# A gated DeltaNet and Mamba-2 decoder step on one core: GpSimd's order of halves and masks in the GDN loop is changed

## What is computed

```python
a_mat = einsum("bnhid,bnhjd->bnhij", k * beta, k) * decay * strict
t_mat = triangular_solve(eye + a_mat, eye, lower=True, unit_diagonal=True)   # the inverse
u = t_mat @ (v * beta);  w = t_mat @ (k * beta * exp(g))
...
v_new = u_c - w_c @ S
o = qd_c @ S + qk_c @ v_new
S = S * exp(gl_c) + kd_c.T @ v_new
```

## Time and profile before

| | us |
|---|---|
| median of 3 runs | 2419.1 (2417.37 to 2422.41) |
| profiled execution, its own time | 2417.6 |
| its span in the trace | 2415.8 |
| PE busy | 2326.3 |
| POOL busy | 1794.2 |
| DVE busy | 1614.2 |
| ACT busy | 1276.5 |

### The profile page before, as it was taken

One profiled execution on the slowest core, in us unless ns is written; L12 is line 12 of the kernel. 1 busy time (PEld: TensorE's weight loads), 2 busy tenths in 40 slices (PEclk: granted clock), 3 DMA queues, 4 the chain that ended last, 5 costly groups with the idle time before them and its releaser, 6 DMA issues.

```text
span 2415.8 us, 59306 instructions
## 1 busy us (share of the span) xinstructions
PE 2326.3 (96%) x21792; PEld 2183.8 (90%) x21792; DVE 1614.2 (67%) x3159; ACT 1276.5 (53%) x2236; POOL 1794.2 (74%) x2284
## 2 busy tenths in 40 slices
PE   5899999999999999999999979999999999999997
PEld 5799999999999999989999978999999999899997
DVE  7667666666666676761217576998999989703375
ACT  4555555555555555543335456555555555433453
POOL 5566566565555556558889968888898889798896
PEclk9999999999999999999999989999999999999999
DMA  5444444444444444436444446766576657454443
GB/s 200 154 155 151 157 155 151 149 150 145 146 154 149 145 144 147 145 125 223 149 167 151 158 148 211 228 202 206 199 245 215 194 196 239 174 195 157 153 156 118
DMA packets 126776, 410.89 MB, mean 170 GB/s; under 512 B 21344, under 2 KB 37984, under 8 KB 122112
## 3 DMA queue, kind: packets, MB, share of 16 engines
q1 hardware_dynamic: 80784, 294.49, 35.2%
q10 hardware_dynamic: 45936, 115.64, 14.1%
HBM read 363.47 MB, written 46.61 MB: 170 GB/s over the span
## 4 chain that ended last, share of the span: by engine, by line
POOL 37%; PE 34%; issue 22%; DVE 4%; ACT 1%; POOLq 0%; DMA 0%; DVEq 0%; ACTq 0%
POOL wl L336 36%; PE psj L381 10%; PE psj L383 10%; PE psj L382 10%; POOL h L344 1%; PE psA L773 1%; PE psE L403 1%; PE psE L747 1%; PE psA L721 1%; DVE h L2012 0%; DVE arena L1535 0%; DVE xl L1819 0%; DVE xl L1460 0%; PE psB L727 0%; ACT xh L845 0%
## 5 line engine op out<-in xcount | busy, mean ns | idle before, releaser
L336 POOL TENSOR_TENSOR wl<-ring,wh 128x256 fp32r<-128x256 f32 x2232 | 1760.9, 824 | 600.4 <-ACT wh L826 599.8
L381 PE MATMUL psj<-xh,wh 128*128 128x288 f32 x4400 | 1357.9, 309 | 31.7 <-DVE xl L1460 16.5
L382 PE MATMUL psj<-xl,wh 128*128 128x288 f32 x4400 | 1305.7, 297 | 0.0
L383 PE MATMUL psj<-xh,wl 128*128 128x288 f32 x4400 | 1301.0, 296 | 0.0
L381 PEld LDWEIGHTS psj<-xh,wh 128*128 128x128 f32 x4400 | 831.3, 189 | 83.1 <-issue 43.9
L826 ACT ACTIVATE wh<-ring 128x1024 fp32r<-128x1024 f32 x558 | 586.5, 1059 | 583.8 <-PE psj L383 535.1
L382 PEld LDWEIGHTS psj<-xl,wh 128*128 128x128 f32 x4400 | 833.7, 189 | 1.9
L383 PEld LDWEIGHTS psj<-xh,wl 128*128 128x128 f32 x4400 | 834.6, 190 | 0.0
L907 ACT ACTIVATE arena<-psj 128x256 f32<-128x256 f32 x112 | 42.7, 381 | 190.7 <-PE psj L383 185.0
L1811 DVE TENSOR_TENSOR h<-h,psj 128x288 f32 x32 | 14.6, 455 | 155.7 <-PE psj L383 155.7
L1885 DVE SCALAR_TENSOR_TENSOR arena<-arena 128x256 f32<-128x256 f32 x144 | 110.7, 796 | 3.4
(11 more groups left out here) (346 smaller groups left out, 2965.4 us busy)
## 6 DMA issues: line engine op xcount, KB each, us to landing
ring<-weights_d SPq DMA_DIRECT2D x558, 512.0 KB, 3.3
h<-gstate_d ACTq DMA_DIRECT2D x16, 1024.0 KB, 6.1
gst_s_d<-h ACTq DMA_DIRECT2D x16, 1024.0 KB, 3.9
h<-sstate_d ACTq DMA_DIRECT2D x32, 512.0 KB, 5.4
sst_s_d<-h ACTq DMA_DIRECT2D x32, 512.0 KB, 5.0
arena<-g_rows_d ACTq DMA_DIRECT2D x16, 864.0 KB, 6.0
arena<-s_rows_d ACTq DMA_DIRECT2D x8, 1152.0 KB, 8.6
h_spill_d<-h ACTq DMA_DIRECT2D x2, 2304.0 KB, 7.5
```

Of the source, the lines that this page charges most:

```text
L336: ins = pool.tensor_tensor(wl[:, s, n:n + 2], ring[:, s, n:n + 2], wh[:, s, n:n + 2].bitcast(F32), ALU.subtract)
L381: pe.matmul(out, w_h, xh[:, kt, :], start=(kt == 0), stop=False)
L382: pe.matmul(out, w_h, xl[:, kt, :], start=False, stop=False)
L383: mm = pe.matmul(out, w_l, xh[:, kt, :], start=False, stop=(kt == KT - 1))
```

## The change

Two things in GpSimd's program for the GDN loop. The sample masks are written ahead of the fifth half of weights (k=4), not behind it. And ahead of the seventh half (k=6) GpSimd waits until VectorE has ended the inverse of the same iteration (`g_de` at m * 6 + 6). This wait stands in the loop over m = 0 to 14; the last iteration is written out behind the loop, without it. GpSimd computes the same things from the same data.

```diff
             pool.wait_ge(S("spill"), 16)
-            with pool.Fori(0, GH) as m:
+            def gdn_halves(m, hold):
+
                 for k in range(12):
                     hc = 2 * T_GLOOP + k
-                    lower(m * 12 + (hc + 1), hc % 4)
                     if k == 4:
                         sample_masks(m)
+                    if hold and k == 6:
+                        pool.wait_ge(S("g_de"), m * 6 + 6)
+                    lower(m * 12 + (hc + 1), hc % 4)
+
+            with pool.Fori(0, GH - 1) as m:
+                gdn_halves(m, True)
+            gdn_halves(GH - 1, False)
             at = 2 * T_GLOOP + 12 * GH
```

## The result

| | before | after |
|---|---|---|
| median, us | 2419.1 (2417.37 to 2422.41) | 2448.58 (2446.8 to 2451.8) |
| profiled execution, its own time | 2417.6 | 2451.8 |
| its span | 2415.8 | 2450.0 |
| period of the GDN loop | 62.94 | 64.23 to 64.27; five of 65.8 |
| rest of TensorE before L545 / L552, start to start | 0.22 | 1.84, 15 times |

The ratio of after to before is 1.0121, with a 95% interval of 1.011 to 1.0132: slower by 29.5 us. The lines of the kernel after are 7 higher than those of before: L545 is now L552, L1618 is L1625, L1703 is L1710, L1609 is L1616, L1533 and L1535 are L1540 and L1542, and L383 is L390.

A forecast was written before the change was run, and what follows sets the result against it. TensorE, busy for 96% of the span, was taken to bound the kernel. -4.6 + 30.2 + 4.5 = +30.1 us on the profiled 2417.6 gave 2447.7, and 2449 us as median; range 2428 to 2467.

The forecast's parts named there:

- The masks at no cost: Masks ahead of half 4: it ends some 2.1 us later, covered by 7.7 us or more before TensorE's e=16; cost nothing.
- Level 3, -4.6: With GpSimd still, TensorE's gap at inverse level 3 shrinks from 0.55 to 0.22 us in 14 iterations: -4.6 us.
- The taps, +30.2: Behind the inverse, GpSimd's twelve instructions stretch VectorE's q/k conv taps; L545 starts 2.01 us later in 15 iterations: +30.2 us.
- The pairing of the prologue: In the prologue the same ten VectorE instructions, beside unbroken GpSimd work, take 7.39 us against 2.33 alone; taken for the loop.
- Rival 3: A smaller stall behind the inverse: two copies escape GpSimd, stall 0.9 us, 2428 us, range 2418 to 2440; chance 0.17.
- The clock, +4.5: TensorE's longer rest before L545 drops its clock in one iteration of five: 3 x 1.5 = +4.5 us; bounds 0 and 23.
- What is late next, hidden: Later halves, SP's refill and taps j=2,3 (some 0.9 us late) stay hidden from TensorE; if not, up to 13 us more.
- The sum: All terms together: +30.1 us on the profiled 2417.6 gives 2447.7; the median, 1.5 above, 2449 us.
- That the clock falls in most iterations: Rival: 10 to 15 falls of TensorE's clock give +15 to +23 in place of 4.5, 2459 to 2468 us; chance 0.11.
- That the taps hide: Rival: taps end by 186.99, stretched by less than 3.05 us, L545 doesn't wait, only -4.6 stays: 2414.5 us; chance 0.08.
- Strict turns: Rival: each of the ten taps waits for a whole GpSimd instruction, 9.33 us, stall 3.95, +55, 2474 us; chance 0.02.

The follow-up runs named there:

- e4_hold_to_level4: The change, with the hold ahead of the seventh half ended earlier, by VectorE's mask of inverse level 4: 2415.75 us, ratio 0.9987 to the kernel before.
- e5_hold_to_rss: The change, with the hold ended later, by the VectorE pair that releases TensorE at e=23: 2426.88 us, ratio 1.0031 to the kernel before.
- e1_masks_only: The kernel before with the sample masks ahead of the fifth half and no hold: 2420.9 us, ratio 1.0009.
- e3_hold_eighth: The change, with the hold ahead of the eighth half (k=7) in place of the seventh: 2423.52 us, ratio 1.0022 to the kernel before.

## Why the prediction held, point by point

**The masks at no cost.** Right for the loop: 62.93 to 62.98 us a period with the masks ahead alone. Not complete: the cover that I named is that of TensorE at e=16, and I did not look at what GpSimd's pause before the fifth half was worth to VectorE in the first iteration. The masks fill this pause, and a copy that is kept waiting is then kept 2 us longer. That it is kept waiting isn't given: it happened in the profiles of the change, `e4_hold_to_level4` and `e5_hold_to_rss`, and not in those of `e1_masks_only` and `e3_hold_eighth`. How much of it is in the median stays open. All four pairs of kernels that differ in the masks' place have the one with the masks ahead at the higher median, by 1.1 to 2.4 us; against the kernel before of their own runs it is 0 to 2.2 us. The largest, of the masks alone, has an interval of 1.0 to 1.0018, and all its 11 executions are above the median of the kernel before. So a price of 1 to 2 us is likely, and the "nothing" was probably that much too low; no profile shows where it lies.

**Level 3, -4.6.** Right in place, size and count: 0.22 us in 14 iterations, 0.61 left in the last. The runs with the hold to level 4 show it as a gain by itself.

**The taps, +30.2.** The mechanism is shown, by the 12, 8 and no instructions beside the taps. The size was too large: 15 x 1.62 = 24.3. The pairing of the prologue, 7.39 us, was the nearest row there was, but in the loop the first copy escapes: it starts at 188.17, 0.03 us ahead of GpSimd, and takes 0.17 us. So 6.80 us, 0.59 less. Two links of the chain were 0.10 longer each than I had them: 194.97 to 195.10 from the taps to L1710 (I took 0.03), and 195.80 to 195.95 from there to L552 (0.05). 2.01 - 0.59 + 0.20 = 1.62. Rival 3 named this escape for both copies; it happened for one.

**The clock, +4.5.** Five falls where I chose three, each of 1.56 us where I had 1.5: 7.8 us.

**What is late next, hidden.** Right. No second stall at e=24 or e=27. The taps j=2 and 3 take 3.17 us from 195.84, where the earlier trace rows had 3.59 beside GpSimd's own half 8. They end 3.06 us behind the start of L552 and ended 2.31 behind that of L545: 0.75 late, where I had 0.9. ScalarE now waits for them, and TensorE doesn't (timeline of ACT):

```profile
199.68 0.68 ACT L959 ACTIVATE arena<-arena 128x576 f32<-128x576 f32 x1 [0.77 <-DVE arena L1542]
```

**The sum.** 24.3 - 4.6 + 7.8 = 27.5 where I had 30.1. The hold alone measured 29.0 (2447.47 - 2418.47), the change 29.5. So 1.5 to 2 us are in none of my terms; in the profile of the hold alone, 27.6 of 28.8 us lie in the first stall and the 14 periods behind it, as the terms have it. The 2449 is nearer to the measured 2448.58 than its terms deserve: one was 5.9 too large, one 3.3 too small, and the first iteration was not in it. That is luck. In the profiled execution alone, whose first rest was 4.48 longer, the time was 2451.8.

**The rivals.** That the clock falls in most iterations: no, in a third. That the taps hide: true of the kernel held to level 4, not of this one. Strict turns: the ten instructions would have taken 9.3 us and took 6.80. GpSimd's twelve took 8.96 us in that row, only 0.56 above 12 x 0.70, so most of VectorE's own 2.33 us passed while GpSimd was at work. The Trainium skill (SBUF — State Buffer, "Who interferes with whom") names the right instructions; beside these rows its "fully blocks" is too strong as a price. That it is a port which the two engines share, no run here tests.

## What to carry to other kernels

A hold is judged by its end, not by its start: an event that releases two engines at once builds the collision that the hold was to avoid, and here the same hold, ended some 6 us earlier by a count that was there already, turned a loss of 29.5 us into a gain of 2.7, and of 4.4 with the masks behind the fifth half. List what both engines do in the 10 us behind the release, and how much slack stands ahead of the next thing that the bounding engine waits for. A loop's first and last iteration want their own reading, since the hold of the sixth half cost 1.9 us over the 14 steady periods and 4.95 in the last one, as profiled.

## What the runs showed of the hardware

**A small VectorE copy can wait through a whole row of GpSimd instructions.** The copy of 128x16 floats took 0.17 us alone and 6.84 us beside about ten unbroken instructions of 0.7 us (83.86 to 90.67). In the other profiles without a hold in the first iteration it took 0.18 to 0.83; a second copy took 0.21 to 0.23, once 1.63 and twice 6.38. Each of the four long waits ended when GpSimd paused. Rows of 23 instructions without a pause also stood beside copies of 0.2 us, so the row is not enough for the wait. The Trainium skill (SBUF — State Buffer, "Who interferes with whom") has it that the one that issues first gets the shared pair; in this trace, at 83.86, the copy came while GpSimd was at work, and several later instructions of GpSimd went ahead of it. In the loop, where VectorE had a queue of such instructions ready, ten took 6.80 us, about one of GpSimd's 0.70 each.

**An instruction with an input in PSUM was not stretched.** The pair L1710 took 0.70 us at 195.10, in the midst of GpSimd's row (188.20 to 197.16), and 0.70 with GpSimd still, at 191.28 in the kernel held to `g_rss`.

**Rests of equal length don't all cost the clock.** Of 15 rests of 1.84 us, at equal work in between, 5 were followed by 3.41 us at the 1.2 GHz level and 10 by none, in the change and in the kernel with the hold alone. Rests of 0.50 us were followed by none. Of the first rests of 2.81 to 2.87 us, in the five kernels with a hold in the first iteration, three were followed by 3.41 us at this level and two by none.
